# RWKV scan on TensorE: inner tensors in the opposite partition half, products on all four 64x64 quarters, diagonal and off-diagonal groups interleaved

## The chip, the cores and the metric

The kernel runs on one core of one Trainium2 chip. Its time is the device time of one execution in microseconds (us). A core has TensorE (PE, with its weight loads shown apart as PEld), VectorE (DVE), ScalarE (ACT), GpSimd (POOL) and the DMA queues. Each engine works through its own list of instructions in order and waits on semaphores where it needs another one's result.

## The reference

The whole kernel is a chain of a two-layer block (Fourier mix, gated linear attention, attention, convolutional FFN) and a second block (RWKV-7, HGRN, a mixture of 64 experts). The change touches only the RWKV-7 scan of the second block, eight heads of width 64, in two directions, over 256 tokens of context and 512 of latent:

```python
def _rwkv7_scan(r, w, k, v, a, b, s0, reverse, emit):
    def step(s, inp):
        r_t, w_t, k_t, v_t, a_t, b_t = inp
        sa = jnp.einsum('bhvk,bhk->bhv', s, a_t)
        s = s * w_t[:, :, None, :] + sa[..., None] * b_t[:, :, None, :] + v_t[..., None] * k_t[:, :, None, :]
        y = jnp.einsum('bhvk,bhk->bhv', s, r_t) if emit else None
        return s, y
...
```

All is in float32.

## The kernel before

`rwkv_scan` works in chunks of 64 tokens: 12 chunks in each of two directions, `N` = 24 items, the directions in turn. The first four items of each direction are context and give no output; from item 8 on, the items give output (`emit`). A chunk's 64 steps are rewritten as products of 64x64 matrices: the scores of a chunk (`pq`), the inverse of a triangular matrix built by repeated squaring (`sq`, `q4`, `q8` for the powers; `r1`, `r2`, `r3` for the inverse R of the 16-blocks; `xh`, `g` and `R4` extend it), the right-hand side (`w`), its solution in two goes (`u1`, `t`, `w2`, `u2`), the transposes of the next operands (`bk`, `v`), and output and state (`y`, `zt`, `z`).

The eight heads are held as four pairs p, one head of a pair in partitions 0 to 63 and the other in 64 to 127 (h = 0 and 1, `H[h]`). One group of products, written by `each`, is 8 matmuls of 64x64: for each p, first h = 0, then h = 1. Both operands and the result of a product lie in the same half, so h = 0 uses rows 0 to 63 and columns 0 to 63 of the array, and h = 1 the other diagonal quarter. A float32 product becomes two matmul and two weight-load instructions, so a group of 8 shows as x16 in the profile. Groups with 128 moving columns are `sk` (L2347) and `r1` (L2356).

The work is pipelined over rounds r = -1 to 25. In round r TensorE does the scores of item r + 1, the inverse of item r, keys, `xh`, `g` and transposes of item r - 1, and right-hand side, solution and output of item r - 2. The order within a round is written out by hand: TensorE runs `first` to `fifth`, ScalarE its list of copies out of PSUM (L2478), VectorE its adds and masks (L2527 is the add). Waits between the engines are by counted semaphores; `after("w2", r - 1)` lets the engine go on when `w2` has been counted r - 1 times. The lines the profile shows:

| line | what |
|---|---|
| L2326, L2327 | `sq`, two groups; L2326 opens a round |
| L2338, L2340 | `w` = A_hat z + AR v, accumulated, two groups' worth |
| L2347 / L2356 | `sk` / `r1`, 128 columns |
| L2359, L2366, L2371 | `q4`, `u1`, `rb` |
| L2380, L2382, L2389, L2390, L2397 | `r2`, `q8`, `xh` twice, `t` |
| L2404, L2410, L2416 | `u2` (waits for `w2`), `g`, `r3` |
| L2421, L2422, L2429, L2437 | `pq` twice, `v`, `bk` (two groups) |
| L2448 to L2459 | `y`: the state's update, and with output three groups more |
| L2478 | every ScalarE copy PSUM to SBUF |
| L2527, L2537, L2539, L2603 | VectorE: add; masks `pm` and `em`; first output copy |

## Time and profile before

| what | value |
|---|---|
| median of 3 runs | 3609.66 us (3606.34 to 3609.83) |
| the profiled execution | span 3608.5 us from the first to the last instruction; its own time has no separate figure, and the span lies 1.2 us below the median of the runs |
| TensorE busy / weight loads / VectorE / ScalarE | 92% / 62% / 41% / 26% |
| RWKV scan | from about 2062 us; TensorE busy 93.75 of the 100 us from 2085 |

Times are from the start of the span. A timeline row gives the start of a run of equal instructions, the time from the first one's start to the last one's end, the engine, the line, the shape and the count, and in brackets how long the engine had been idle and which instruction released it.

### The profile page before, as it was taken

To read this page: it belongs to the slowest core of one execution; us is meant where nothing else is said; L and a number is where in the kernel's file an instruction comes from. 1 tells how busy PE (TensorE), PEld (TensorE's weight loads), DVE (VectorE), ACT (ScalarE), POOL (GpSimd) and SP (SyncE) were. 2 spreads that over 40 slices of the span, in tenths; PEclk is the share of its full clock that TensorE was granted. 3 is DMA by queue.
4 is the path that set the end of the run, shared out by engine and by line. 5 is a ranking of instruction groups with operands and counts; after the bars stand their busy time and mean duration, and the time that the engine had idled before them with its cause. 6 is when DMAs were issued, how large, how long until landed. Compare 5 with 4: busy or idle time off the path is not lost. (4 is left out here: it accounts for less than half of the span.)

```text
span 3608.5 us, 67939 instructions
## 1 busy us (share of the span) xinstructions
PE 3331.8 (92%) x27542; PEld 2255.2 (62%) x27542; DVE 1472.6 (41%) x3002; ACT 920.5 (26%) x1782; POOL 776.5 (22%) x727
## 2 busy tenths in 40 slices
PE   7999999999999999999999599989988899999984
PEld 3557555555555687787865289965775466655543
DVE  1213443345322454445266834434455233333324
ACT  2122232222002343222121433234322122222211
POOL 0000332223510024335410000003311233333320
PEclk9999999999999999999999599989999999999996
DMA  5330133312111003532211000001102799999996
GB/s 225 123 112 25 48 124 155 148 51 83 56 39 65 30 13 140 226 136 103 84 59 36 0 4 4 4 17 53 65 26 81 284 357 357 358 360 349 359 386 233
DMA packets 97639, 485.23 MB, mean 134 GB/s; under 512 B 16915, under 2 KB 21043, under 8 KB 53249
## 3 DMA queue, kind: packets, MB, share of 16 engines
q1 hardware_dynamic: 80880, 443.66, 33.4%
q0 software_dynamic: 16528, 38.25, 3.2%
q8 instruction: 176, 2.88, 0.3%
q14 instruction: 55, 0.44, 0.0%
HBM read 466.90 MB, written 31.46 MB: 138 GB/s over the span
## 5 line engine op out<-in xcount | busy, mean ns | idle before, releaser
L1011 PE MATMUL psum<-arena 128*128 128x384 f32 (+1 forms) x2464 | 674.4, 434 | 6.3 <-ACT arena L600 5.3
L1011 PEld LDWEIGHTS psum<-arena 128*128 128x128 f32 x2464 | 463.7, 189 | 221.3 <-issue 23.8
L842 PE MATMUL psum<-arena 128*128 128x256 f32 (+1 forms) x1904 | 511.6, 431 | 23.3 <-PEq L3092 10.0
L842 PEld LDWEIGHTS psum<-arena 128*128 128x128 f32 x1904 | 363.6, 191 | 171.8 <-issue 27.3
L3623 PE MATMUL psum<-arena 128*64 128x256 f32 x3072 | 352.6, 378 | 15.8 <-DMA arena<-exp_w_in 13.2
L3623 PEld LDWEIGHTS psum<-arena 128*64 128x64 f32 x3072 | 231.8, 134 | 161.4 <-issue 54.1
L453 POOL TENSOR_TENSOR arena<-arena 128x512 f32<-128x512 f32 x66 | 88.0, 1334 | 1054.9 <-POOLq L1671 365.7
L1139 DVE SCALAR_TENSOR_TENSOR arena<-arena 128x511 f32<-128x511 f32 (+1 forms) x264 | 177.0, 713 | 138.1 <-ACT arena L1117 135.0
L1089 ACT ACTIVATE arena<-psum 128x384 f32<-128x384 f32 (+1 forms) x176 | 76.3, 435 | 510.5 <-PE psum L1011 510.1
L462 POOL TENSOR_TENSOR arena<-arena 128x512 f32<-128x512 f32 (+1 forms) x74 | 114.6, 1549 | 395.6 <-PE psum L1011 245.6
L3637 PE MATMUL psum<-arena 128*64 128x512 f32 x768 | 185.3, 601 | 0.6 <-DMA arena<-exp_w_in 0.6
L1133 DVE TENSOR_TENSOR arena<-psum,arena 128x384 f32<-128x384 f32 (+1 forms) x132 | 64.6, 490 | 283.3 <-PE psum L1011 283.3
L2478 ACT ACTIVATE arena<-psum 128x256 f32<-128x256 f32 (+1 forms) x264 | 104.0, 422 | 240.2 <-PE psum L2327 62.1
L2796 PE MATMUL psum<-arena 128*128 128x384 f32 (+1 forms) x560 | 161.3, 449 | 4.1 <-ACT arena L600 4.0
L3717 DVE SCALAR_TENSOR_TENSOR arena<-arena,psum 128x128 f32<-128x128 f32 (+1 forms) x97 | 33.8, 349 | 281.0 <-ACT arena L3674 281.0
L563 POOL TENSOR_TENSOR arena<-arena 128x1536 f32<-128x1536 f32 (+1 forms) x3 | 11.3, 3766 | 636.3 <-ACT arena L600 636.3
L2796 PEld LDWEIGHTS psum<-arena 128*128 128x128 f32 x560 | 106.6, 191 | 59.5 <-ACT arena L600 7.9
L1336 PE MATMUL psum<-arena 128*128 128x512 f32 x272 | 140.7, 598 | 1.1 <-ACT arena L600 1.1
L3545 POOL TENSOR_TENSOR arena<-arena 128x1 f32<-128x1 f32 x195 | 39.8, 204 | 394.0 <-DVE arena L3712 379.4
L2039 PE MATMUL psum<-arena 128*128 128x512 f32 x240 | 116.6, 592 | 0.8 <-ACT arena L600 0.8
L2527 DVE TENSOR_TENSOR arena<-psum,arena 128x256 f32<-128x256 f32 x128 | 53.6, 424 | 130.7 <-PE psum L2459 39.5
L3562 POOL DMA_INDIRECT yrows<-arena x96 | 98.5, 1026 | 37.3 <-issue 37.3
(516 smaller groups left out, 5199.3 us busy)
## 6 DMA issues: line engine op xcount, KB each, us to landing
arena<-exp_w_in SPq DMA_DIRECT2D x207, 1024.0 KB
arena<-w_mod_r_in SPq DMA_DIRECT2D x72, 1024.0 KB, 7.0
arena<-w_ffn_up_in SPq DMA_DIRECT2D x44, 1024.0 KB, 4.8
arena<-w_ffn_down_in SPq DMA_DIRECT2D x32, 704.0 KB, 4.2
arena<-yrows SPq DMA_DIRECT2D x8, 2048.0 KB, 16.5
arena<-w_hgrn_in SPq DMA_DIRECT2D x10, 1024.0 KB
arena<-w_even_in_in SPq DMA_DIRECT2D x17, 512.0 KB, 3.6
arena<-w_in_in SPq DMA_DIRECT2D x15, 512.0 KB, 3.6
```

What stands on the lines that cost most here:

```text
L453: pool.tensor_tensor(s1, a21, a22, ADD).then_inc(s["ws"], 1)
L462: pool.tensor_tensor(a12, a12, self.piece(m, p, 5), SUB).then_inc(s["ws"], 1)
L842: mm = pe.matmul(pair_bank(ps, q, x, h), lhsT[:, k, :], rhs[:, k, :], start=(k == 0 and x in (1, 2, 7)), stop=(k == KH - 1), skip_group_ch ...
L1011: return pe.matmul(pair_bank(ps, q, x, h), feed.weights(m, q, x)[:, k, :], b.moving(x)[:, k, :], start=(k == 0 and x in (1, 2, 7)), stop=( ...
L1139: last = dve.scalar_tensor_tensor(y, x[:, lo + a:hi + e], column(q, v, tap), y, MUL, ADD)
L1336: pe.matmul(ps[:, 2 * b, :], lhsT, m["A"][:, x, 0:LAT], start=(x == 0), stop=(x == KD - 1))
L2039: mm = pe.matmul(ps[:, 2 * b, :], lhsT, m["A"][:, k, 0:LAT], start=(k == 0), stop=(k == KD - 1))
L2478: return act.activation(dst, src, ACT.Copy)
L2796: mm = pe.matmul(pair_bank(ps, i, x, h), lhsT[:, k, :], rhs[:, k, :], start=(k == 0 and x in (1, 2, 7)), stop=(k == 3), skip_group_check=x ...
L3562: pool.indirect_dma_start(io["yrows"], bass.IndirectOffsetOnAxis(ap=ids[:, u:u + 1].bitcast(U32), axis=0), y[u], None, bounds_check=LAT * ...
L3623: mm = pe.matmul(ps[64 * c:64 * c + 64, 0, 0:256], xt[u][:, k, :], wgu[w][:, k, :, c * P:(c + 1) * P], start=(k == 0), stop=(k == KD - 1))
L3637: mm = pe.matmul(ps[64 * c:64 * c + 64, 4, :], hT[:, j * 64:(j + 1) * 64], wdn[w][:, j, c * 512:(c + 1) * 512], start=(j == 0), stop=(j == 1))
```

## The change

Every product now has a form: `same` (result in the operands' half) or `turned` (result in the other half, so the product uses an off-diagonal quarter). The scores `pq` are turned, so the squared powers P and Q, R and its extensions R16 and R32, `EE`, and also `AR`, `RB`, `bkT`, `vT`, `Wb` and U lie in the half opposite to their head; the chunk's inputs, `XH`, the state z and the output stay in their own half. `side_by_side` takes two groups and issues them in turn: for each p, group a with h = 0 and 1, then group b with h = 0 and 1. Where both are there, one is in its own half and the other is turned, and they write to different PSUM banks.

The order of a round is rewritten as 15 steps of such pairs or single groups. The accumulations `w` and `y` are taken apart: their terms are issued in several steps. Two semaphores, `wz` and `y3`, make TensorE wait for its own earlier step before the other half of the array writes to the same bank. `t` goes to bank 7 and U's second part to bank 7's first half; `q4c` is split in `q4c` and `p4c`. ScalarE's list swaps two pairs of copies. VectorE's list moves the masks `pm` and `em` forward and puts `R3` and `r0` behind the output and `zt`. The number of products, copies and adds stays. Step by step, in an output round: (1) second `sq` | A_hat z; (2) first `sq` | `rb`; (3) AR v | `sk`; (4) `q4` | first `pq`; (5) `u1` | `xh`; (6) `r1` | `xh`; (7) `t` | `bk`; (8) second `pq`; (9) z r_hat | `bk`; (10) `q8` | bkT v; (11) `r2` | v AR; (12) `u2` | `g`; (13) `v`; (14) U RB; (15) `r3` | bkT U.

```diff
-           "y zt yc z init")
+           "y zt yc z init wz y3 p4c")
+def side_by_side(a, b):
+    made = [None, None]
+    for p in range(4):
+        for u, step in enumerate((a, b)):
+            if step is not None:
+                for h in range(2):
+                    made[u] = step(p, h)
+    return made
...
+    def twos(b):
+        return ps[:, b, :].rearrange("p (a b c) -> p a b c", a=4, b=2)
     def out(b, h, p, half=0):
         return ps[H[h], b, half * W4 + p * C:half * W4 + (p + 1) * C]
-
-    def each(step):
-        for p in range(4):
-            for h in range(2):
-                mm = step(p, h)
-        return mm
...
+            def same(b, lhsT, rhs, half=0):
+                return lambda p, h: pe.matmul(out(b, h, p, half), lhsT(p, h), rhs(p, h), start=True, stop=True)
+            def turned(b, lhsT, rhs, half=0):
+                return lambda p, h: pe.matmul(out(b, 1 - h, p, half), lhsT(p, h), rhs(p, h), start=True, stop=True)
+            def of(x):
+                return lambda p, h: x[H[h], p, :]
+            def hats(which, j):
+                return lambda p, h: hat(which, j, p, h)
+            def unit(p, h):
+                return ident[H[h], H[h]]
+            def adding(b, lhsT, rhs, half, h_out, first, end):
+                return lambda p, h: pe.matmul(out(b, h ^ h_out, p, half), lhsT(p, h), rhs(p, h), start=first and p == 0, stop=end,
+                                              skip_group_check=True)
+            def wide_keys(j):
+                n = (2 if item(j)[2] else 1) * C
+                return lambda p, h: pe.matmul(ps[H[1 - h], 1, 2 * p * C:2 * p * C + n], hat(RW_K_HAT, j, p, h), a_and_r(j, p, h),
+                                              start=True, stop=True)
+            def wide_rp():
+                return lambda p, h: pe.matmul(ps[H[h], 4, 2 * p * C:2 * (p + 1) * C], Q2[H[h], p, :], RP[H[h], p, :, :],
+                                              start=True, stop=True)
+            def values(j):
+                c = item(j)[1]
+                v = at(RW_V, 4, T)[:, :, c * C:(c + 1) * C]
+                return lambda p, h: v[H[h], p, :]
+            pe.wait_ge(s["init"], 2)
+            for r in range(-1, N + 2):
+                A, B, K, L = active(r), active(r - 1), active(r - 2), active(r + 1)
+                emit_b, emit_k = B and item(r - 1)[2], K and item(r - 2)[2]
+                d = r % 2
+                back = (r - 2) % 2
+                P16, Q16 = of(PQ16[:, 0, :, :]), of(PQ16[:, 1, :, :])
+                p2, r_now = of(RP[:, :, 1, :]), of(RP[:, :, 0, :])
+                if A:
+                    after("pm", r + 1)
                     after("vc", r - 1)
...
+                if K:
+                    after("z", r - 3)
                     after("xc", r - 1)
...
+                sq, wz = side_by_side(same(3, Q16, P16, 1) if A else None,
+                                      adding(5, hats(RW_A_HAT, r - 2), of(z[d]), 0, 1, True, False) if K else None)
+                if K:
+                    wz.then_inc(s["wz"], 1)
+                if emit_b:
+                    after("R4", r - 1)
+                sq, rb = side_by_side(same(3, P16, Q16) if A else None,
+                                      turned(2, hats(RW_B_HAT, r - 1), hats(RW_R_HAT, r - 1)) if emit_b else None)
+                if A:
+                    sq.then_inc(s["sq"], 1)
+                if emit_b:
+                    rb.then_inc(s["rb"], 1)
+                if K:
+                    after("ak", r - 1)
+                    after("vc", r - 1)
+                    after("wz", r - 1)
+                if B:
                     after("zt", r - 2)
                     after("yc", r - 10)
...
+                w, sk = side_by_side(adding(5, of(AR[back][:, :, 0, :]), of(vT[back]), 0, 0, False, True) if K else None,
+                                     wide_keys(r - 1) if B else None)
+                if K:
+                    w.then_inc(s["w"], 1)
+                if B:
+                    sk.then_inc(s["sk"], 1)
+                if A:
+                    after("q2", r + 1)
+                    after("bc", r - 1)
+                if L:
+                    after("em", r + 1)
+                q4, pq = side_by_side(same(6, p2, of(Q2)) if A else None,
+                                      turned(0, hats(RW_A_HAT, r + 1), hats(RW_B_HAT, r + 1), 1) if L else None)
+                if A:
+                    q4.then_inc(s["q4"], 1)
+                if K:
+                    after("wc", r - 1)
+                    after("R4", r - 1)
+                    after("uc", r - 2)
+                if B:
                     after("R3", r)
...
+                    after("wc", r - 1)
+                u1, xh = side_by_side(same(7, of(R32), of(Wb)) if K else None, turned(5, of(R16), unit) if B else None)
+                if K:
+                    u1.then_inc(s["u1"], 1)
+                if A:
+                    after("r0", r + 1)
+                    after("R3", r)
+                if B:
+                    after("em", r)
+                r1, xh = side_by_side(wide_rp() if A else None,
+                                      turned(5, of(EE[(r - 1) % 3][:, 1, :, :]), of(R16), 1) if B else None)
+                if A:
+                    r1.then_inc(s["r1"], 1)
+                if B:
+                    xh.then_inc(s["xh"], 1)
+                if K:
+                    after("u1c", r - 1)
+                if B:
+                    after("q4c", min(r + 1, N))
+                t, bk = side_by_side(same(7, of(EE[(r - 2) % 3][:, 0, :, :]), of(U), 1) if K else None,
+                                     turned(6, hats(RW_B_HAT, r - 1), unit) if B else None)
+                if K:
+                    t.then_inc(s["t"], 1)
+                if L:
+                    pq = side_by_side(None, turned(0, hats(RW_B_HAT, r + 1), hats(RW_A_HAT, r + 1)))[1]
+                    pq.then_inc(s["pq"], 1)
+                if K:
+                    after("ak", min(r, N))
+                    after("zt", r - 2)
+                    after("yc", r - 10)
+                y3, bk = side_by_side(adding(1, of(z[d]), hats(RW_R_HAT, r - 2), 1, 0, True, False) if emit_k else None,
+                                      turned(6, hats(RW_K_HAT, r - 1), unit, 1) if B else None)
+                if emit_k:
+                    y3.then_inc(s["y3"], 1)
+                if B:
+                    bk.then_inc(s["bk"], 1)
+                if A:
+                    after("q4c", r + 1)
+                    after("p4c", r + 1)
+                if K:
                     after("bc", r - 1)
...
+                    after("y3", r - 9)
+                q8, y = side_by_side(same(3, of(P4), of(Q4)) if A else None,
+                                     adding(1, of(bkT[back][:, 1, :, :]), of(vT[back]), 0, 1, not emit_k, False) if K else None)
+                if A:
+                    q8.then_inc(s["q8"], 1)
+                if A:
+                    after("R1", r + 1)
+                r2, y = side_by_side(same(4, of(Q4), r_now) if A else None,
+                                     adding(1, of(vT[back]), of(AR[back][:, :, 1, :]), 1, 1, False, False) if emit_k else None)
+                if A:
+                    r2.then_inc(s["r2"], 1)
+                if K:
+                    after("w2", r - 1)
+                if B:
+                    after("xc", r)
+                    after("rbm", r - 8)
+                u2, g = side_by_side(same(7, of(R32), of(Wb)) if K else None,
+                                     turned(2, of(XH[:, 0, :, :]), of(XH[:, 1, :, :])) if B else None)
+                if K:
+                    u2.then_inc(s["u2"], 1)
+                if B:
+                    g.then_inc(s["g"], 1)
+                if B:
                     after("q8c", min(r + 1, N))
...
+                    v = side_by_side(None, turned(3, values(r - 1), unit))[1]
+                    v.then_inc(s["v"], 1)
+                if K:
+                    after("uc", r - 1)
+                    after("rbm", r - 9)
+                if emit_k:
+                    side_by_side(None, adding(1, of(U), of(RB[back]), 1, 1, False, True))
+                if A:
+                    after("q8c", r + 1)
+                    after("R2", r + 1)
+                r3, y = side_by_side(same(4, of(Q8), r_now) if A else None,
+                                     adding(1, of(bkT[back][:, 0, :, :]), of(U), 0, 1, False, True) if K else None)
+                if A:
+                    r3.then_inc(s["r3"], 1)
+                if K:
+                    y.then_inc(s["y"], 1)
...
-                    copy(Q2, bank(3, 0))
-                    copy(RP[:, :, 1, :], bank(3, 1)).then_inc(s["q2"], 1)
+                    copy(RP[:, :, 1, :], bank(3, 1))
+                    copy(Q2, bank(3, 0)).then_inc(s["q2"], 1)
                 if active(r - 2):
                     after("w", r - 1)
                     after("u2", r - 2)
@@ -2491,24 +2533,24 @@
                     after("q4", r + 1)
                     after("r2", r)
                     after("q8", r)
-                    copy(Q4, bank(6, 0))
-                    after("R1", r + 1)
-                    copy(P4, ps[:, 4, :].rearrange("p (a b c) -> p a b c", a=4, b=2)[:, :, 1, :]).then_inc(s["q4c"], 1)
+                    copy(Q4, bank(6, 0)).then_inc(s["q4c"], 1)
                 if active(r - 2):
                     after("u1", r - 1)
                     after("y", r - 2)
                     copy(U, bank(7, 0)).then_inc(s["u1c"], 1)
                 if active(r):
-                    after("q8", r + 1)
-                    copy(Q8, bank(3, 0)).then_inc(s["q8c"], 1)
+                    after("R1", r + 1)
+                    copy(P4, twos(4)[:, :, 1, :]).then_inc(s["p4c"], 1)
                 if active(r - 1):
                     after("xh", r)
                     after("g", r - 1)
                     copy(flat(XH), bank(5)).then_inc(s["xc"], 1)
+                if active(r):
+                    after("q8", r + 1)
+                    copy(Q8, bank(3, 0)).then_inc(s["q8c"], 1)
                 if active(r - 2):
                     after("u2", r - 1)
-                    after("t", r - 1)
-                    copy(U, bank(7, 1)).then_inc(s["uc"], 1)
+                    copy(U, bank(7, 0)).then_inc(s["uc"], 1)
...
+                    add(Wb, 7, Wb, 1).then_inc(s["w2"], 1)
+                if L:
+                    after("pq", r + 2)
+                    after("sq", r + 1)
+                    dve.tensor_tensor(PQ16, pq, mask((r + 1) % 2, 0), MUL).then_inc(s["pm"], 1)
+                if A:
+                    after("r2", r + 1)
+                    after("R1", r + 1)
+                    add(R, 4, R).then_inc(s["R2"], 1)
+                if B:
                     after("g", r)
                     after("u2", r - 1)
                     after("R3", r)
                     add(R32, 2, R16).then_inc(s["R4"], 1)
+                if L:
+                    after("t", r - 1)
+                    dve.tensor_tensor(EE[(r + 1) % 3], pq, mask((r + 1) % 2, 1), MUL).then_inc(s["em"], 1)
+                if K:
+                    d, c, _ = item(r - 2)
+                    after("y", r - 1)
+                    if emit_k:
+                        dst = Y[:, :, c * C:(c + 1) * C]
+                        if r - 2 < 16:
+                            dve.tensor_scalar(dst, bank(1, 1), 1.0, None, MUL).then_inc(s["yc"], 1)
+                        else:
+                            add(dst, 1, dst, 1).then_inc(s["yc"], 1)
+                    after("z", r - 3)
+                    add(zt, 1, z[d]).then_inc(s["zt"], 1)
+                if A:
                     after("r3", r + 1)
                     after("R2", r + 1)
                     after("xh", r)
                     after("R4", r)
+                    add(R16, 4, R).then_inc(s["R3"], 1)
+                if L:
+                    after("pm", r + 2)
+                    after("r3", r + 1)
+                    after("R3", r + 1)
+                    dve.tensor_tensor(R, PQ16[:, 0, :, :], repeat(eye, 4), ADD).then_inc(s["r0"], 1)
+                if K:
+                    d, c, _ = item(r - 2)
+                    after("zt", r - 1)
                     end = last[:, d, :, c:c + 1].to_broadcast([P, 4, C])
                     dve.tensor_tensor(z[d], zt, end, MUL).then_inc(s["z"], 1)
 
```

## Rows read from the trace of the kernel before

**Rows 1.** The page: the span, busy time of the engines, DMA share by fortieths.

```profile
span 3608.5 us, 67939 instructions
...
PE 3331.8 (92%) x27542; PEld 2255.2 (62%) x27542; DVE 1472.6 (41%) x3002; ACT 920.5 (26%) x1782; POOL 776.5 (22%) x727
...
DMA  5330133312111003532211000001102799999996
```

**Rows 2.** Windows in and around the scan: window, its length, busy us (instructions) per engine.

```profile
core 0: us, PE busy (x) PEld busy (x) DVE busy (x) ACT busy (x) POOL busy (x), PEclk, DMA share, GB/s
2062.00:2065.00 3.00, 2.04 (x34) 1.85 (x35) 0.85 (x3) 0.00 (x0) 0.00 (x0) 0.50 0.00 0
...
2085.00:2185.00 100.00, 93.75 (x2982) 91.68 (x2979) 41.06 (x90) 35.42 (x90) 0.00 (x0) 1.00 0.02 4
...
2355.75:2369.95 14.20, 13.67 (x438) 13.54 (x436) 5.95 (x13) 4.32 (x11) 0.00 (x0) 1.00 0.02 3
```

**Rows 3.** Timeline, TensorE: the first group of rounds 0, 2, 9, 10 and 23.

```profile
2064.94 1.12 PE L2326 MATMUL psum<-arena 64*64 64x64 f32 x16 [0.87 <-DVE arena L2537]
...
2085.62 0.63 PE L2326 MATMUL psum<-arena 64*64 64x64 f32 x16
...
2172.37 0.63 PE L2326 MATMUL psum<-arena 64*64 64x64 f32 x16
...
2185.18 0.63 PE L2326 MATMUL psum<-arena 64*64 64x64 f32 x16
...
2369.95 0.63 PE L2326 MATMUL psum<-arena 64*64 64x64 f32 x16
```

**Rows 4.** Timeline of round 11, with output: groups, copies and adds.

```profile
2202.12 1.04 PE L2356 MATMUL psum<-arena 64*64 64x128 f32 x16
...
2203.00 0.63 PE L2359 MATMUL psum<-arena 64*64 64x64 f32 x16
...
2203.46 0.64 PE L2366 MATMUL psum<-arena 64*64 64x64 f32 x16
2203.68 0.94 ACT L2478 ACTIVATE arena<-psum 128x256 f32<-128x256 f32 x3 [1.83 <-PE psum L2359]
...
2206.51 0.60 ACT L2478 ACTIVATE arena<-psum 128x512 f32<-128x512 f32 x1 [0.55 <-PE psum L2390]
2206.98 0.42 DVE L2527 TENSOR_TENSOR arena<-psum,arena 128x256 f32<-128x256 f32 x1 [1.44 <-PE psum L2397]
...
2207.46 0.68 PE L2404 MATMUL psum<-arena 64*64 64x64 f32 x16 [0.53 <-DVE arena L2527]
...
2210.06 0.69 DVE L2537 TENSOR_TENSOR arena<-psum,arena 128x512 f32<-128x512 f32 x1 [0.42 <-PE psum L2422]
...
2210.66 0.68 DVE L2539 TENSOR_TENSOR arena<-psum,arena 128x512 f32<-128x512 f32 x1
...
2213.79 0.42 DVE L2527 TENSOR_TENSOR arena<-psum,arena 128x256 f32<-128x256 f32 x1 [2.11 <-PE psum L2459]
...
2214.13 0.41 DVE L2603 TENSOR_SCALAR arena<-psum 128x256 f32<-128x256 f32 x1
```

**Rows 5.** Timeline, TensorE, other stages: column halves, full width, column quarters.

```profile
start us, us, engine line op out<-in xcount [idle before <-releaser]
...
3001.81 3.64 PE L3623 MATMUL psum<-arena 128*64 128x256 f32 x32
...
3006.46 0.64 PE L3499 MATMUL psum<-arena 128*64 128x5 f32 x16
3006.95 1.50 PE L3637 MATMUL psum<-arena 128*64 128x512 f32 x6
...
2474.81 5.65 PE L2796 MATMUL psum<-arena 128*128 128x384 f32 x17
...
118.34 1.07 PE L224 MATMUL psum<-arena 128*32 128x512 f32 x8
```

**Rows 6.** Window on L224, column quarters: its first instructions.

```profile
118.30:118.36 0.07, 0.03 (x4) 0.03 (x4) 1.00 0.00 0
```

More of the change, by code:

```diff
@@ L2319, in after @@
                     pe.wait_ge(s[sem], count)
-            def first(r):
-                if active(r):
-                    j = r
-                    after("pm", j + 1)
-                    after("vc", r - 1)
-                    each(lambda p, h: pe.matmul(out(3, h, p), PQ16[H[h], 0, p, :], PQ16[H[h], 1, p, :], start=True, stop=True))
-                    each(lambda p, h: pe.matmul(out(3, h, p, 1), PQ16[H[h], 1, p, :], PQ16[H[h], 0, p, :], start=True, stop=True)
-                         ).then_inc(s["sq"], 1)
-                if active(r - 2):
-                    j = r - 2
-                    d = j % 2
-                    after("z", j - 1)
-                    after("ak", j + 1)
-                    after("vc", j + 1)
-                    after("xc", r - 1)
-                    for p in range(4):
-                        for h in range(2):
-                            pe.matmul(out(5, h, p), hat(RW_A_HAT, j, p, h), z[d][H[h], p, :], start=True, stop=False)
-                        for h in range(2):
-                            mm = pe.matmul(out(5, h, p), AR[j % 2][H[h], p, 0, :], vT[j % 2][H[h], p, :], start=False, stop=True)
-                    mm.then_inc(s["w"], 1)
-                if active(r - 1):
-                    j = r - 1
-                    n = (2 if item(j)[2] else 1) * C
@@ L2432, in fifth @@
-            def fifth(r):
-                if active(r - 1):
-                    j = r - 1
-                    after("q4c", min(r + 1, N))
-                    for half, which in enumerate((RW_B_HAT, RW_K_HAT)):
-                        mm = each(lambda p, h: pe.matmul(out(6, h, p, half), hat(which, j, p, h), ident[H[h], H[h]],
-                                                         start=True, stop=True))
-                    mm.then_inc(s["bk"], 1)
-                if active(r - 2):
-                    j = r - 2
-                    d, _, emit = item(j)
-                    after("uc", j + 1)
-                    after("bc", j + 1)
-                    after("w2", j + 1)
-                    for p in range(4):
-                        for h in range(2):
-                            pe.matmul(out(1, h, p), bkT[j % 2][H[h], 0, p, :], U[H[h], p, :], start=True, stop=False)
-                        for h in range(2):
-                            mm = pe.matmul(out(1, h, p), bkT[j % 2][H[h], 1, p, :], vT[j % 2][H[h], p, :], start=False, stop=True)
-                    if emit:
-                        after("rbm", j - 7)
-                        for p in range(4):
-                            for h in range(2):
-                                pe.matmul(out(1, h, p, 1), z[d][H[h], p, :], hat(RW_R_HAT, j, p, h), start=True, stop=False)
-                            for h in range(2):
-                                pe.matmul(out(1, h, p, 1), U[H[h], p, :], RB[j % 2][H[h], p, :], start=False, stop=False)
-                            for h in range(2):
-                                mm = pe.matmul(out(1, h, p, 1), vT[j % 2][H[h], p, :], AR[j % 2][H[h], p, 1, :],
-                                               start=False, stop=True)
-                    mm.then_inc(s["y"], 1)
@@ L2463, in _ @@
-            pe.wait_ge(s["init"], 2)
-            for r in range(-1, N + 2):
-                first(r)
-                second(r)
-                third(r)
-                fourth(r)
-                fifth(r)
+                w, sk = side_by_side(adding(5, of(AR[back][:, :, 0, :]), of(vT[back]), 0, 0, False, True) if K else None,
[4 more added lines that the diff above has]
+                    sk.then_inc(s["sk"], 1)
@@ L2530, in mask @@
                 return masks[:, d, which, :].rearrange("p (k a c) -> p k a c", k=2, a=1).to_broadcast([P, 2, 4, C])
[L2532 to L2543 removed]
+            pq = ps[:, 0, :].rearrange("p (k a c) -> p k a c", k=2, a=4)
+            R = RP[:, :, 0, :]
             for d in range(2):
@@ L2571, in _ @@
                     dve.tensor_tensor(RB[j % 2], bank(2, 0), repeat(masks[:, j % 2, 2, C:2 * C], 4), MUL).then_inc(s["rbm"], 1)
-                if active(r):
-                    after("r2", r + 1)
-                    after("R1", r + 1)
-                    add(RP[:, :, 0, :], 0, RP[:, :, 0, :]).then_inc(s["R2"], 1)
-                if active(r - 2):
+                if K:
                     after("t", r - 1)
```

132 lines of the change are left out of this document (11 added, 121 removed).

## The prediction

> **What bounds the kernel now.** I read the page's head first [rows 1]: TensorE is busy for 92% of the 3608.5 us span. That is an average over many stages, so next I asked for the stretches that hold the changed function, the RWKV scan [rows 2]. It starts at about 2062, and round 23 of its rounds starts at 2369.95 [rows 3]. Between 2085 and 2185 TensorE is busy for 93.75 of 100 us, VectorE for 41 and ScalarE for 35, and the DMA share is 0.02: TensorE is the bound, the two copying engines run at under half, and no transfer is hidden behind this stage. What the scan saves, the end of the kernel saves too.
>
> Then the rounds. The first matmul of a round (L2326) marks its start [rows 3]. Rounds 2 to 8, in which no chunk gives output, take (2172.37 - 2085.62) / 7 = 12.39 us; round 9 takes 12.81; rounds 10 to 22, with output, take (2369.95 - 2185.18) / 13 = 14.21.
>
> Inside a round [rows 4] the unit is a group of 8 products of 64 columns, 16 matmul instructions. One group starts 0.465 us after the one before (2203.46 against 2203.00), 0.029 us per instruction, though one instruction lasts 0.218: the start-to-start distance is what a group costs. A group of 128 columns costs 0.88 (2202.12 to 2203.00). An output round has 25 narrow groups and 2 wide ones: 25 x 0.467 + 2 x 0.88 = 13.4. Most of the other 0.8 us is one wait, for `w2` ahead of L2404 (0.53 idle beyond the tail of the group before it). So 14.2 us is a queue of groups back to back, and only fewer or shorter groups shorten it.
>
> **What the change removes and adds.** The products themselves stay: 25 narrow and 2 wide groups. What moves is which quarter of the array each uses and in what order. Today every product stays in its half (rows h, columns h), so two diagonal quarters work and two rest. The new order puts 24 of the 27 groups into 12 steps, each with one diagonal and one off-diagonal group, instruction by instruction in turn; 3 groups stay alone (second `pq`, `v`, U with `RB`). Without output it is 9 steps and 5 lone groups. ScalarE's and VectorE's instructions keep their number and sizes; the two new TensorE waits (`wz`, `y3`) are costed below. So the disputed number is what such a step costs. The trace has no row with all four quarters at work; I bound it from both sides.
>
> Upper bound without a penalty for turning: no overlap, 2 x 0.468 = 0.936. Lower bound: all four quarters work together, the price of one group, 0.468 (a step with a wide group: 0.88). What the rows say [rows 5]:
> - At full width, 17 instructions of 384 columns span 5.65 us, so 0.324 each (the last one's tail of some 0.47 taken off), 0.216 for 256. With two column halves, 32 instructions of 256 columns span 3.64: (3.64 - 0.38) / 31 = 0.105. Two halves that share all 128 rows, with different streams, do overlap fully. This reads two streams from every partition, just as four quarters would.
> - Column quarters (L224) [rows 5, 6]: 8 instructions of 512 columns, 0.43 each at full width, span 1.07, and four had started within the first 0.03 us. So four tiles at once is possible, and instructions can start 7 ns apart when they go to different tiles.
> - The diagonal pair: 64 columns would be 0.324 x 64 / 384 = 0.054 per instruction, and they come every 0.029. So rows and columns that differ overlap too.
>
> What no row shows is two row halves that send results to the same column half at once. The change keeps the two groups of a step in different PSUM banks and waits on `wz` and `y3` where a bank changes quarters. I take the lower bound, 0.468: three kinds of concurrency are in the rows, and the fourth is the product of two of them.
>
> [...]
>
> **The sum.** With shorter steps the copies between products come into the open, so I walked the new order instruction by instruction, with prices from [rows 4]: a result can be read 0.21 us after the next step could start (2203.00 + 0.465 to 2203.68); a ScalarE copy takes 0.38 and the next can start 0.28 after it (three in 0.94), the long one takes 0.60; VectorE 0.42 and 0.33, long 0.69 and 0.60; TensorE goes on 0.06 after a copy's end (2206.98 + 0.42 to 2207.46). On the old order the walk gives 14.15 and 12.33 for the measured 14.21 and 12.39, so the prices hold.
>
> On the new order an output round's 15 steps start at 0, 0.47, 1.02, 1.90, 2.56, 3.02, 3.90, 4.37, 4.84, 5.52, 5.99, 6.46, 6.92, 7.58 and 8.04, and the next round at 8.51. Work is 13 x 0.468 + 2 x 0.88 = 7.84; waits are 0.09 (third step, for `zt`), 0.18 (fifth, for the copy of `Wb`), 0.21 (tenth, `y3`, TensorE waiting for itself), 0.18 (fourteenth, the last copy of U). `z` is ready 2.1 us into the next round but needed only a round later, since the two directions alternate; behind each TensorE wait the whole step is queued, and that is in the walk. VectorE's 6 and ScalarE's 4.3 busy us per round still fit in 8.5, so neither becomes the bound. A round without output comes to 7.61 (13 x 0.468 + 0.88 + 0.46 for `q2` + 0.18).
>
> Savings: rounds 0 and 1 together 4.2; seven rounds x (12.39 - 7.61) = 33.5; round 9, 12.81 - 7.74 = 5.1; thirteen x (14.21 - 8.51) = 74.1; the last three about 7. Sum 124; the walk on both orders gives 122.7, as round 10 and the slow-clock start fill and drain differently. I take 123. The profiled span of 3608.5 lies 1.2 below the median of 3609.66, the same 1.2 stays around it: 3609.7 - 123 = **3487 us**.
>
> Of the terms that are uncertain: a step of 0.44 gives -130, of 0.50 -113 (four starts 7 ns apart fit in 0.058, the distance at which one quarter takes its next instruction, so little is to be lost); results visible at 0.26 in place of 0.21 give -118. The granted clock is 0.50 at the start of the scan and 1.00 from 2085 on [rows 2]. [...]
>
> **Rivals.**
> 1. *The feed of instructions becomes the bound.* No row has matmuls with a weight load each that come faster than one in 0.028 for long: even with 5 columns (L3499) 16 take from 3006.46 to 3006.95, 0.031 each. That may be the 64-column weight load or the feed; a full step needs 0.0146. Somewhere between, say at 0.022, a step costs 0.70, the round about 11 and the saving 70: 3540. Four starts in 0.03 us speak against it, but those may have been queued.
>    [...]
> 2. *No overlap beyond two quarters* (shared outputs or loads serialise, or the feed is already at its limit of 0.029): steps of 0.936. The walk then gives 13.86 and 11.36, because the long wait at L2404 is gone, and 14 us in all: 3596.
> 3. *Slower: each turn from diagonal to off-diagonal lets the array run dry.* An instruction lasts 0.218 while its successor comes after 0.058 on its quarter, so a turn could cost 0.16; eight turns in a step are 1.3 us, on some 264 steps 340 us: about 3935. It decides from 14 / 264 / 8 = 7 ns per turn. Against it: today's groups turn between two quarters all the time and lose nothing.
> 4. *The change doesn't do what it says*, if both groups of a step fell on the same quarters. In the code each step pairs one output in its own half with one in the other half, all in different banks; this would end as rival 2.
>
> **Chances.** All four quarters, 3475 to 3510: 0.62. Feed-bound between, 3510 to 3580: 0.17. Nothing beyond two, 3590 to 3600: 0.09. Within 0.2%, 7 us, which is about what a measurement of this kernel can tell: 0.02. Slower: 0.10. So faster 0.88, same 0.02, slower 0.10. The range takes the first case and most of the second: 3475 to 3578.
>
> **What would show it.** The distance of round starts: 8.5 and 7.6 (right), 11 to 12 (feed), 13.9 and 11.4 (no overlap), over 14.3 (turns). Inside a step, 32 matmuls from start to next step: 0.47, 0.94, or more. TensorE's waits should be for `zt`, `Wb`, U and `y3`, each about 0.2. ScalarE and VectorE busy time stays within 2%, over a shorter stage. If the round is longer than 8.5 with steps at 0.47, a chain of copies was priced too low; then the wait after `q2` or `wc` should be the long one.

## The result, and the profile after

The changed kernel takes **3580.6 us** (median of 4 runs, 3577.6 to 3584.9) beside 3608.0 for the kernel before on the same chip: ratio 0.9927, 95% interval 0.9915 to 0.9939. It is faster, by 27 us; 123 were forecast, and the forecast range, 3475 to 3578, ends just below it. The sign was right, the size was not.

The head of the page of the profile after, against [rows 1]. ScalarE and VectorE do the same work, as forecast:

```profile
span 3580.3 us, 67966 instructions
...
PE 3235.4 (90%) x27542; PEld 2148.4 (60%) x27542; DVE 1467.1 (41%) x3002; ACT 920.1 (26%) x1782; POOL 777.3 (22%) x727
```

The windows after, columns as in [rows 2]:

```profile
2062.00:2085.00 23.00, 19.31 (x512) 18.18 (x512) 8.33 (x18) 5.45 (x15) 0.00 (x0) 0.65 0.01 4
2085.00:2185.00 100.00, 71.43 (x3266) 65.80 (x3268) 43.25 (x97) 37.16 (x97) 0.00 (x0) 1.00 0.02 4
2185.00:2370.00 185.00, 130.92 (x5936) 120.14 (x5936) 77.32 (x177) 59.67 (x151) 0.00 (x0) 0.99 0.02 4
```

TensorE's busy time between 2085 and 2185 falls from 93.75 to 71.43 us, yet it gets through only 6534 matmuls and weight loads there where it got through 5961: 9.6% more. It stands idle for more than a quarter of the time, and VectorE and ScalarE are still under half.

Rounds after, by the start of VectorE's `em` mask (L2621), once per round:

```profile
2092.32 0.68 DVE L2621 TENSOR_TENSOR arena<-psum,arena 128x512 f32<-128x512 f32 x1
...
2159.16 0.68 DVE L2621 TENSOR_TENSOR arena<-psum,arena 128x512 f32<-128x512 f32 x1
...
2184.90 0.68 DVE L2621 TENSOR_TENSOR arena<-psum,arena 128x512 f32<-128x512 f32 x1
...
2347.00 0.68 DVE L2621 TENSOR_TENSOR arena<-psum,arena 128x512 f32<-128x512 f32 x1
```

Six rounds without output take 66.84, 11.14 each (before 12.39, forecast 7.61); twelve with output take 162.10, 13.51 each (14.21, forecast 8.51). The scan, from its first to its last matmul, falls from 339.8 to 314.7 us.

Inside a round the trace shows two things. First, TensorE's matmuls in a step of two groups (L2330 is `same`, L2333 `turned`, L2345 `adding`, L2350 and L2354 the wide ones); the rows are the start of one step, the end of it and the start of the next:

```profile
2200.22 0.25 PE L2330 MATMUL psum<-arena 64*64 64x64 f32 x2
2200.26 0.22 PE L2333 MATMUL psum<-arena 64*64 64x64 f32 x2
...
2200.63 0.25 PE L2330 MATMUL psum<-arena 64*64 64x64 f32 x2
2200.67 0.22 PE L2333 MATMUL psum<-arena 64*64 64x64 f32 x2
...
2201.06 0.27 PE L2345 MATMUL psum<-arena 64*64 64x64 f32 x2 [0.16 <-issue]
```

Pairs of each form follow one another every 0.058 us, so the step's 32 matmuls pass in 0.47: all four quarters work at once, at the price forecast. Second, TensorE stops, mostly in the middle of a step, and waits for no other engine:

```profile
2201.56 0.49 PE L2350 MATMUL psum<-arena 64*64 64x128 f32 x5
2203.02 0.32 PE L2350 MATMUL psum<-arena 64*64 64x128 f32 x2 [0.97 <-issue]
...
2205.27 0.33 PE L2330 MATMUL psum<-arena 64*64 64x64 f32 x5
2207.20 0.27 PE L2330 MATMUL psum<-arena 64*64 64x64 f32 x1 [1.60 <-issue]
```

The waits of TensorE's weight loads from 2085 to 2370 (engine, line, releaser: us in total, times, longest):

```profile
PEld psum L2330 <- issue: 32.2, 41, 2.0
PEld psum L2333 <- issue: 32.0, 23, 2.4
PEld psum L2345 <- issue: 19.3, 22, 1.6
PEld psum L2354 <- issue: 6.7, 5, 1.6
PEld psum L2350 <- issue: 3.2, 3, 1.2
PEld psum L2330 <- ACT arena L2520: 3.2, 11, 0.6
```

Before, the longest such group in this stretch was `u2` waiting for VectorE, and "issue" was not in the list:

```profile
PEld psum L2404 <- DVE arena L2527: 13.9, 21, 0.7
PEld psum L2380 <- ACT arena L2478: 3.0, 7, 0.4
```

So 93 us of the stage are idle time for which no engine is to blame. That is close to what is missing from the forecast (123 - 27 = 96), but the match alone proves nothing: e1_seq below takes the same time with 63 us of such idle. What remains is the engine's own instruction stream. The DMA view has a queue of that kind, whose packets have 16,384 bytes each; from 2085 to 2185 it moved (queue, kind: packets, MB, share), after and then before:

```profile
q8 instruction: 26, 0.43, 1.7%
```

```profile
q8 instruction: 24, 0.39, 1.7%
```

The scan's 19,712 matmuls and weight loads arrive in 78 such packets of 16,384 bytes, 253 in each. With the 334 separate wait instructions that is 257 a packet. The trace's records give the number itself: from 2085 to 2370 TensorE stands still for over 0.6 us 69 times, and 66 of the 68 distances between these stops are exactly 256 of its instructions, waits included, the other two 512. So a block holds 256, which is 64 bytes each. Without the waits between them, the two long stops above are 251 instructions apart. Between 2196 and 2212 blocks start at 2196.51, 2200.63, 2204.42 and 2208.34, each takes 0.95 to 1.42 us to land, and TensorE stops at about the time of a landing and goes on at 2199.24, 2203.02, 2207.20 and 2211.09, 1.3 to 1.6 us after it. Over the stage the blocks come 3.9 us apart on average, at best 3.3.

The packets' own times in the trace say the same for the whole stretch. 73 blocks start from 2085 to 2370. After 71 of the first 72 TensorE stands still and goes on 1.15 to 1.58 us after the landing, and two such points are about 252 matmuls and loads apart. In the mean a block lands in 1.11 us, TensorE goes on 1.38 later, and the next block starts 1.41 after that, never while TensorE stands: 3.90 in all. So the transfer is less than a third of the distance between blocks. In the kernel before, the blocks come 4.2 us apart, and TensorE's longest waits there name another engine (the rows above).

That is theory **F**, read from this trace: TensorE is fed 256 instructions at most every 3.3 to 3.9 us, 13 to 15 ns each, 26 to 31 ns per matmul with its load, whatever quarters they use. Its rivals were **Q** (the quarters overlap badly, or turning between them costs time), **C** (the chain of copies sets the round) and, for what a wait costs, **W** (each wait instruction has a price of its own, not hidden in the block). The step of 0.47 us above already speaks against Q, and the 3.2 us of waits for ScalarE against C.

### The profile page after: what moved, and what is told of

Its sections match the earlier page's. It is cut to its first block and busy times, and to the rows that moved or that the text cites. A ratio compares the mean times of both kernels' runs of the same rounds, so it can differ in the third digit from the quotient of the medians.

```text
span 3580.3 us, 67966 instructions
## 1 busy us (share of the span) xinstructions
PE 3235.4 (90%) x27542; PEld 2148.4 (60%) x27542; DVE 1467.1 (41%) x3002; ACT 920.1 (26%) x1782; POOL 777.3 (22%) x727
## 5 line engine op out<-in xcount | busy, mean ns | idle before, releaser
L2330 PE MATMUL psum<-arena 64*64 64x64 f32 x3456 | 142.4, 226 | 34.5 <-issue 27.1
L2333 PE MATMUL psum<-arena 64*64 64x64 f32 x3328 | 129.6, 224 | 46.4 <-issue 27.7
L2330 PEld LDWEIGHTS psum<-arena 64*64 64x64 f32 x3456 | 123.9, 138 | 42.2 <-issue 34.1
L2333 PEld LDWEIGHTS psum<-arena 64*64 64x64 f32 x3328 | 115.5, 136 | 51.4 <-issue 32.0
L1336 PE MATMUL psum<-arena 128*128 128x512 f32 x272 | 140.7, 598 | 1.0 <-ACT arena L600 1.0
```

Source lines behind the costliest of these rows:

```text
L1336: pe.matmul(ps[:, 2 * b, :], lhsT, m["A"][:, x, 0:LAT], start=(x == 0), stop=(x == KD - 1))
L2330: return lambda p, h: pe.matmul(out(b, h, p, half), lhsT(p, h), rhs(p, h), start=True, stop=True)
L2333: return lambda p, h: pe.matmul(out(b, 1 - h, p, half), lhsT(p, h), rhs(p, h), start=True, stop=True)
```

## The experiments

The first four ran beside one another (before: 3606.7), as did the next four (3607.2) and the last two (3608.8). The table gives the time, the length of the scan, and for 2085 to 2185 the number of matmuls and weight loads, the blocks and the granted clock:

| kernel | us | ratio (interval) | scan us | instr. | blocks | clock |
|---|---|---|---|---|---|---|
| before | 3608.0 | 1 | 339.8 | 5961 | 24 | 1.00 |
| after | 3580.6 | 0.9927 (0.9915-0.9939) | 314.7 | 6534 | 26 | 1.00 |
| e5_after_again | 3579.4 | 0.9926 (0.9913-0.9940) | 311.0 | 6459 | 26 | 1.00 |
| e1_seq | 3579.0 | 0.9918 (0.9902-0.9935) | 313.9 | 6403 | 25 | 1.00 |
| e2_more_waits | 3645.6 | 1.0107 (1.0090-1.0124) | 374.6 | 5515 | 23 | 0.82 |
| e3_before_more_waits | 3724.6 | 1.0326 (1.0309-1.0344) | 453.8 | 4188 | 17 | 0.89 |
| e4_thin_partners | 3584.6 | 0.9940 (0.9923-0.9957) | 308.4 | 6483 | 26 | 1.00 |
| e6_fewer_waits | 3571.9 | 0.9904 (0.9889-0.9919) | 304.1 | 6852 | 27 | 1.00 |
| e7_fewer_waits_in_turn | 3567.3 | 0.9888 (0.9872-0.9903) | 301.9 | 6936 | 27 | 1.00 |
| e8_after_half_instructions | 3438.8 | 0.9533 (0.9519-0.9548) | 171.6 | 6181 | 25 | 0.50 |
| e9_before_half_instructions | 3453.3 | 0.9566 (0.9550-0.9582) | 183.3 | 5664 | 23 | 0.88 |
| e10_after_half_in_turn | 3439.2 | 0.9529 (0.9513-0.9545) | 169.3 | 6186 | 25 | 0.55 |

**e1_seq: no interleaving.** Only the order of issue inside a step changes:

```diff
-    for p in range(4):
-        for u, step in enumerate((a, b)):
+    for u, step in enumerate((a, b)):
+        for p in range(4):
```

> The changed kernel, but in each step the whole first group is issued before the second: no mixing of diagonal and off-diagonal instructions, same waits, same number of instructions. Theory F (feed): TensorE gets its instructions in blocks of 256, one block in about 3.9 us, 15.2 ns per instruction, whatever the quarters do. Both groups one after the other cost 0.936 per step by the walk (rounds of 13.86 and 11.36), the feed asks 13.5 and 11.1, so the result lies at or a little above the larger: rounds 13.8 to 14.3 and 11.3 to 12.2, 3585 to 3600 us. Rival Q (the quarters overlap badly or turning costs time, and that is what ate the gain): without the turns inside a step the time falls or stays, under 3580. Rival C (the chain of copies bounds the round): the time grows by all that the steps grow, some 5 us a round, to 3650 and more.

The time is that of the changed kernel, and 6 us below the range that I had set for F; it meets, at 3579.0, the "under 3580" that I had set for Q. C, which asked for 3650 and more, is out. What decides against Q is the trace. TensorE is busier (81.48 us of 100), and its weight loads' "issue" stops from 2085 to 2370 are shorter by about as much: 63 us in place of 93. Such a stop still follows each block, about 252 matmuls and loads after the last. What the interleaving saves on the array is waited for afterwards. My range for F was too high because the walk let two groups in a row cost 0.936, a round of 13.86: rounds took 13.16 and 11.46, so by that reading groups on different quarters overlap even when one is issued behind the other. Interleaving, one part of the change, brought nothing here.

**e2_more_waits and e3_before_more_waits: more instructions that do nothing.** 64 waits on a semaphore that has long been met open each of the 27 rounds; the compiler packs them into 32 instructions (the page of e3_before_more_waits has 68,803 instructions where the kernel before has 67,939: 864, or 27 x 32, more). These are the lines of e3_before_more_waits; e2_more_waits has the same loop in the changed kernel.

```diff
+                for _ in range(64):
+                    pe.wait_ge(s["init"], 2)
```

> The changed kernel with 64 waits at the head of each TensorE round on a semaphore that has been met since the start; the compiler packs them into 32 instructions per round that occupy no part of the array. Theory F: 27 x 32 = 864 instructions more to fetch, at 15.2 ns each: +13 us. Rivals Q and C: such an instruction is done in a few ns ahead of a stalled queue, under +3 us.

> The same 32 instructions per round in the kernel before. Theory F: an output round has 864 matmul and weight-load instructions and some 20 others, 13.4 us of fetching, against 14.2 measured; 32 more make 13.9, still under it. Non-output rounds 768 + 20 + 32 = 820, 12.5 us against 12.39. So +0 to +5 us, less than half of what the same instructions cost in the changed kernel. If a met wait simply costs its own time in TensorE's queue, both kernels grow alike.

Both are far off: +65 and +118 us. The timeline of e3_before_more_waits shows the price of a met wait directly, at the head of two rounds:

```profile
2200.05 0.72 PE L2326 MATMUL psum<-arena 64*64 64x64 f32 x16 [2.91 <-issue]
...
2217.10 0.71 PE L2326 MATMUL psum<-arena 64*64 64x64 f32 x16 [2.90 <-issue]
```

2.91 us idle (3.09 from start to start beyond the usual distance) for 32 instructions: 91 to 97 ns each. 27 x 3.09 = 83. The other 35 of 118 I put down to the granted clock, an estimate: it is 0.91 on average from 2085 to 2395 where it was 1.00 (0.09 x 310 = 28), and that is only two thirds of a scan that now lasts 454 us. (The recorded text counts 768 instructions in a round without output; there are 23 groups of 32, 736.) In the changed kernel the same 32 cost 65 us / 27 = 2.4 a round and not 3.1, at a clock of 0.82; I take it that a part is hidden where TensorE would have stood still anyway. So these two runs tested F badly: a met wait took 91 to 97 ns here and the feed gives an instruction every 15, so a wait's own time swamps its share of the block. They gave W its figure.

**e4_thin_partners: fewer instructions off the path.** Two of the partner groups (`rb` and `v` x `AR`) are issued for p = 0 only, so 48 of 864 matmuls and loads of an output round are left out, all of them beside a group that stays.

```diff
-            if step is not None:
+            if step is not None and not (p and getattr(step, "thin", False)):
...
-                                      turned(2, hats(RW_B_HAT, r - 1), hats(RW_R_HAT, r - 1)) if emit_b else None)
+                                      thin(turned(2, hats(RW_B_HAT, r - 1), hats(RW_R_HAT, r - 1))) if emit_b else None)
```

> The changed kernel without three quarters of two groups (rb, B_hat with R_hat; and v with AR in the output sum): only the first pair of heads is multiplied, so part of the output sum is left out. Both groups are partners in a step whose other group stays whole, so the array's time per step and the chain of copies stay. Theory F: 48 instructions fewer in each output round, 48 x 15.2 ns = 0.73 us, on some 15 rounds -11 us. Rival C and the walk of the prediction: no change (under 2 us). Rival Q: between, as a few turns are gone.

The time of the whole kernel says nothing here: the output differs, and the experts' stage later moves its data in 17,008 packets in place of 16,528. The scan itself is 6.3 us shorter, output rounds 12.64 in place of 13.51. F gives 48 x 15.2 ns = 0.73 a round, C nothing; 0.87 was measured, or 0.57 beside the 13.21 of e5_after_again, the same kernel as after. That kernel's scan is 3.7 us shorter than after's, and rounds without output, in which nothing is left out, take 11.14, 11.54 and 11.42 in the three. With such scatter this run is weak support.

**e5_after_again, e6_fewer_waits, e7_fewer_waits_in_turn.** At 21 places (the recorded texts say 20) a wait is already covered by an earlier one of TensorE or by a chain through the other engines. These waits are left out in rounds 3 to 22, 185 instructions in all (67,966 on the page of after, 67,781 on that of e6_fewer_waits); e7_fewer_waits_in_turn has the order of e1_seq as well.

```diff
+                few = 3 <= r < N - 1
...
-                    after("z", r - 3)
-                    after("xc", r - 1)
+                    maybe("z", r - 3)
+                    maybe("xc", r - 1)
```

> The changed kernel once more, as the reference for the three kernels beside it: 3580 +/- 3 us, ratio 0.992 to 0.994, scan stage (first to last matmul) 314 to 315 us.

> The changed kernel without 20 TensorE waits that an earlier wait already covers, in rounds 3 to 22; the program has 185 fewer wait instructions on TensorE. F (blocks of 256 instructions come at 3.9 us at the soonest, 15.2 ns each, and a wait's own issue time hides in the slack of its block): 185 x 15.2 ns = 2.8 us less in the scan, so 311 to 313 us. W (each wait costs its own 70 to 97 ns, as the added waits did): 13 to 18 us less, so 297 to 301 us. C (the chain of copies sets the round): no change, 314 to 315.

> As the kernel without the 20 waits, and in each step the whole first group is issued before the second, no interleaving. F: 310 to 313 us in the scan, as with interleaving, since the count of instructions is what matters. C: with no interleaving the first group's result is there earlier, so it may gain a few us: 305 to 312. If four quarters work only because of the interleaving, about 340.

The changed kernel again came out at 3579.4 as expected, its scan at 311.0, below the 314 to 315. Without the waits the kernel takes 7.5 us less than it and the scan 6.9 less: between F (2.8) and W (13 to 18), 40 ns per wait, of which 15 would be its place in the block. The mean distance of blocks from 2085 to 2350 falls from 3.89 to 3.76 us, the least stays at 3.3 to 3.4. So neither price is right by itself: with fewer waits the blocks come sooner, and each wait costs less than the 91 to 97 ns of e3_before_more_waits. With the groups in turn as well it is 12.1 us less than e5_after_again: 3567.3, the best of the kernels that compute everything. The last 4.6 of that are at the edge of what these runs can tell (3564.3 to 3573.8 against 3569.6 to 3573.1). The "issue" stops remain the longest waits of e7_fewer_waits_in_turn (2085 to 2370):

```profile
PEld psum L2330 <- issue: 21.9, 25, 1.4
PEld psum L2333 <- issue: 20.1, 27, 1.7
PEld psum L2345 <- issue: 7.6, 14, 1.0
```

**e8, e9, e10: half the instructions.** Every product of the scan reads only the upper 16 bits of its operands, as bf16; precision is lost, sizes and order stay. A product is then one weight load and one matmul (9856 in the scan in place of 19,712).

```diff
+    def high(x):
+        v = x.bitcast(mybir.dt.bfloat16)
+        return v[:, 1::2] if len(v.shape) == 2 else v[:, :, 1::2]
...
+    def mm16(pe, dst, lhsT, rhs, **how):
+        return pe.matmul(dst, high(lhsT), high(rhs), **how)
...
-                return lambda p, h: pe.matmul(out(b, h, p, half), lhsT(p, h), rhs(p, h), start=True, stop=True)
+                return lambda p, h: mm16(pe, out(b, h, p, half), lhsT(p, h), rhs(p, h), start=True, stop=True)
```

> The changed kernel, in which every product of the scan reads only the upper 16 bits of its operands (the values lose precision, the sizes and the order stay). A product then takes one weight load and one matmul in place of two of each, so the scan has half as many instructions on TensorE. F: the scan falls to 160 to 190 us, of which 10,500 instructions x 15.2 ns = 160 are the floor of the feed; output rounds 6.7 to 8 us. C (the walk with groups at half their length, 0.234 us): 145 us, output rounds 5.8. If a fixed cost per round of another kind held the changed kernel at 13.5 us a round, the scan stays above 230.

> The kernel before, in which every product of the scan reads only the upper 16 bits of its operands, so that a product takes one weight load and one matmul; two diagonal quarters as before. With the same treatment the changed kernel's scan took 171.6 us. F (the old kernel is bound by its two quarters at 0.029 us per matmul, and half the instructions at the same length each leave 0.234 us per group): the walk gives 197 us and output rounds of 8.1; the feed's floor of 160 us binds in few places. Then four quarters save 25 us of 197 (13%), where they saved 25 of 340 (7%) at full precision. If the two quarters were no bound, the scan comes out at 171 to 176, like the changed kernel's.

> The changed kernel with upper halves only, and in each step the whole first group before the second, no interleaving (with interleaving: 171.6 us in the scan). F: with half the instructions the feed binds less, the array more. If consecutive groups on different quarters overlap by themselves, 165 to 173 us, since a first group's result also comes earlier; if interleaving is what makes four quarters overlap once instructions are there, 195 or more, like two quarters.

With the changed order the scan falls to 171.6 us, inside F's 160 to 190 and far above C's 145; output rounds take 7.20, where F said 6.7 to 8 and C 5.8. The windows of the scan, e8_after_half_instructions:

```profile
2062.00:2233.00 171.00, 130.12 (x4912) 105.49 (x4912) 124.98 (x293) 100.85 (x264) 0.00 (x0) 0.50 0.02 4
```

and e9_before_half_instructions:

```profile
2062.00:2245.00 183.00, 126.20 (x4910) 114.23 (x4912) 127.56 (x294) 100.22 (x264) 0.00 (x0) 0.82 0.02 4
```

A round is half as long, but instructions go by at the old rate: 6181 in 100 us, 25 blocks, where the full kernel had 6534 and 26. In e8_after_half_instructions the granted clock is 0.50 from 2062 to 2233 and so in practically all of the scan (TensorE had been idle for 18.6 us before it); in the changed kernel it is 0.65 from 2062 to 2085 and 1.00 in the next 100 us. C's price for a group holds even so: at that clock a quarter takes its next 64-column bf16 matmul after 0.057 us (2151.510, 2151.567, 2151.624), 4 x 0.057 = 0.23 per group. The waits from 2085 to 2190, e8_after_half_instructions and then e9_before_half_instructions:

```profile
PEld psum L2324 <- issue: 21.4, 47, 1.1
PEld psum L2324 <- ACT arena L2527: 12.7, 44, 0.5
```

```profile
PEld psum L2316 <- DVE arena L2534: 17.5, 27, 1.0
PEld psum L2316 <- ACT arena L2485: 13.2, 15, 1.0
...
PEld psum L2316 <- issue: 3.9, 5, 1.1
```

So the changed order is near two limits at once, the feed and the chain of copies; of the old order the waits show the chain of copies above all. The two times differ by only 11.7 us of 183.3 (6%; forecast 25), and not by the quarters alone, as the clocks differ too. The walk had said that the old order is bound by its two quarters here (197 us). It isn't. It took 0.234 us per group, but where the clock is 1.00 matmuls on a quarter start every 0.033 us (2165.8 to 2166.4), 0.13 per group, and the waits are for copies. And e10_after_half_in_turn at 169.3, inside the 165 to 173 expected, shows again that interleaving is worth nothing.

## Why the prediction was wrong

**The bound before.** Right in the main: 14.2 us were groups back to back. What I didn't see is how near the next limit lay. 5961 instructions in 100 us are 24 blocks, one every 4.2 us, and the feed gave one every 3.9 with the changed kernel's mix of waits. By estimate (4.2 against 3.9, 5961 against 6534) there was 7 to 10% to be had from a change that leaves the number of instructions alone, and the scan got 7.4% shorter (339.8 to 314.7).

**The price of a step: the step that failed.** "I take the lower bound, 0.468: three kinds of concurrency are in the rows, and the fourth is the product of two of them." For the array this was right; a full step passes in 0.47. For the stage it was wrong, because the sum multiplied it by 13 steps in a row: 13 x 0.468 + 2 x 0.88 = 7.84 us for 864 instructions is 9.1 ns each, and they arrive at 15.6 (13.51 us / 864). "Four starts in 0.03 us speak against it, but those may have been queued" names the mistake: eight instructions [rows 5, 6] say what a short burst can do, and a stage of 20,000 showed another rate. The missing 5.0 us in each of 13 output rounds and 3.5 in each of seven others make 65 + 25 = 90 of the 96.

A second term stood at nothing without a reason: a wait that is already met. The scan has 334 separate wait instructions on TensorE, 67 more than before the change, though products, copies and adds keep their number. At the 40 ns of e6_fewer_waits all of them come to 13 us, the added ones to 3. This is an estimate, and a part of the 90, not an addition to it.

**Rival 1** was the mechanism, with a chance of 0.17 and a price too low. I set 0.022 per matmul and load, a value between two bounds that no row showed; the scan shows 0.031 (2 x 100 / 6534), near the 0.028 to 0.031 at which all the rows that I had quoted stopped. Its own sentence, "that may be the 64-column weight load or the feed", had the answer: for one pair of quarters it was the array (0.029), and the feed stood right behind. The range took in only most of this rival, and the result lies 3 us above it; that it came so close is no merit of the sum.

Within a step the array was faster than any of these figures: matmuls start every 15 ns (32 in 0.47 us). Two quarters share each half of the rows in such a step, and the 32 matmuls with their loads pass as fast as 16 did in the kernel before, on two quarters that share none (0.465).

**Rival 2** (nothing beyond two quarters: 13.86, 11.36, 3596) lies nearer to the measured round with output than any other, and is still not the cause: steps take 0.47, the waits are "issue", and the stops come once per block. **Rival 3**, an array that drains at each turn, isn't seen: a step with eight turns passes in 0.47, as forecast without a price for them. **Rival 4** is out for the same reason: a step of 0.47 is half of the 0.936 that two quarters take for as many matmuls.

**The waits between engines.** `zt`, `Wb`, U and `y3` were to cost 0.66 a round. TensorE's weight loads wait for ScalarE 3.2 us in the whole stretch. The chain never came to bind, so these runs don't say whether it was priced right.

**The clock.** In the changed kernel 1.00 from 2085 to 2185 and 0.99 to 2370, with stops of up to 2.4 us between; in the kernel before 1.00 in both.

**What stays open.** Of the 3.3 to 3.9 us per block the transfer takes 0.9 to 1.4. Why TensorE goes on only 1.4 us after the landing, and what starts the next block 1.4 us later, isn't settled: no run changed the size of a block or its place. Nor did any run have so few instructions that the feed was out of play, which would show the chain of copies alone.

## What to carry to other kernels

Before spreading small products over more of the array, count instructions. The most matmuls and weight loads that went by here in a window of 100 us were 69 per us (6936 in e7_fewer_waits_in_turn, 27 blocks), and 65 in the changed kernel (6534, 26 blocks); the waits come on top. Look also at how many instruction packets the queue moved. Near that rate the cheaper step on the array, 0.47 in place of 0.936, took 25 us off the scan where 123 were forecast, and issuing the groups in turn changed nothing (e1_seq, 3579.0 against 3580.6). What fewer instructions brought: 185 waits less took 6.9 us off the scan (e6_fewer_waits), one pass in place of two took it from 314.7 to 171.6 (e8_after_half_instructions). Wider products or shared weights would lower the count too; no run here tried them. A short burst in a trace shows what the array can do (32 matmuls in 0.47 us), not what it can be fed: over 100 us a matmul with its load took 0.031.

## What the runs showed of the hardware

- TensorE's instructions come in blocks of 16,384 bytes, 256 instructions each with the waits, 253 of them matmuls and loads. In after they are at best 3.3 us apart and 3.9 on average (2085 to 2370). When they run out, TensorE is idle (in after mostly for 1 to 2 us, at most 2.4), the view of waits says "issue", and it goes on 1.15 to 1.58 us after a block's landing.
- Four 64x64 quarters work at once: in after 32 float32 matmuls of 64 columns, each with its own weight load, pass in 0.47 us, as fast as 16 on two quarters in the kernel before.
- A separate wait instruction that has long been met cost TensorE 91 to 97 ns in e3_before_more_waits, by estimate from 2.91 to 3.09 us for 32; in the changed scan, where TensorE stops for its blocks anyway, leaving 185 out (e6_fewer_waits) saved 40 ns each.
- From 2085 to 2185 the granted clock was 0.82 in e2_more_waits and 0.89 in e3_before_more_waits, and 0.50, 0.88 and 0.55 in e8_after_half_instructions, e9_before_half_instructions and e10_after_half_in_turn, which have half the instructions; by estimate e3_before_more_waits lost some 30 of its 118 us to that.
